# Tokens of a tile in order of their residue of sixteen, and one attention group's probabilities turned on VectorE

## What is computed

```
h = rmsnorm(x);  proj = h @ w_in
branch_a = gated retention, 4 heads (rotary, decay by distance, forward and backward)
branch_b = dilated attention, 3 groups of 8 heads of 64:
    group 1: keys at distance <= 64            (window 128,  step 1)
    group 2: keys at distance <= 256, step 4   (window 512,  step 4)
    group 3: keys at distance <= 1024, step 16 (window 2048, step 16)
    att = sum_g w_g * acc_g / sum_g w_g * l_g    (one softmax over the three)
x = x + (gate0 * branch_a + gate1 * branch_b) @ w_out
h = rmsnorm(x);  16 experts, each takes its best 64 tokens of 512 (SwiGLU), adds into x
return rmsnorm(x)
```

## Time and profile before

| | |
|---|---|
| median of 3 runs | 2398.88 us (2398.83 to 2399.2) |
| the profiled execution | 2399.03 us |
| its span, first to last instruction | 2397.2 us |
| TensorE busy | 2373.5 us (99%) |
| VectorE busy | 1588.7 us (66%) |
| ScalarE busy | 1475.4 us (62%) |
| GpSimd busy | 420.3 us (18%) |
| moved by transfers | 557.21 MB, mean 232 GB/s |
| mean granted TensorE clock | 0.997 of full speed |

### The profile page before, as it was taken

One profiled execution on the slowest core, in us unless ns is written; L12 is line 12 of the kernel. 1 busy time (PEld: TensorE's weight loads), 2 busy tenths in 40 slices (PEclk: granted clock), 3 DMA queues, 4 the chain that ended last, 5 costly groups with the idle time before them and its releaser, 6 DMA issues.

```text
span 2397.2 us, 33849 instructions
## 1 busy us (share of the span) xinstructions
PE 2373.5 (99%) x11840; PEld 1983.3 (83%) x11840; DVE 1588.7 (66%) x1737; ACT 1475.4 (62%) x1705; POOL 420.3 (18%) x287
## 2 busy tenths in 40 slices
PE   8999999999999999999998999999999999999998
PEld 7888888888888888888886888888888888888886
DVE  4444454534545454445346988888888888888887
ACT  5555564533466555544234777777777777777776
POOL 1534434000053334320002000000000000000000
PEclk9999999999999999999999999999999999999999
DMA  6413321225433224122238999999999999999998
GB/s 187 127 45 99 87 74 65 71 96 203 157 93 88 82 61 126 44 83 80 87 149 315 403 392 384 376 390 377 387 390 391 386 387 382 377 387 375 402 377 314
DMA packets 213498, 557.21 MB, mean 232 GB/s; under 512 B 10944, under 2 KB 92480, under 8 KB 208320
## 3 DMA queue, kind: packets, MB, share of 16 engines
q1 hardware_dynamic: 206384, 530.76, 60.1%
q0 software_dynamic: 7056, 25.69, 3.6%
HBM read 533.34 MB, written 23.07 MB: 232 GB/s over the span
## 4 chain that ended last, share of the span: by engine, by line
PE 98%; DVE 1%; DMA 0%; issue 0%; ACT 0%; POOLq 0%; SPq 0%; DVEq 0%; ACTq 0%
PE bank L1361 43%; PE bank L1024 15%; PE bank L1069 13%; PE bank L992 8%; PE bank L1013 6%; PE bank L1044 4%; PE bank L1183 2%; PE bank L1085 2%; PE bank L1407 2%; PE bank L1164 1%; PE bank L1107 1%; PE bank L1144 1%; PE bank L1111 1%; PE bank L1150 1%; PE bank L1241 1%; PE bank L1199 0%
## 5 line engine op out<-in xcount | busy, mean ns | idle before, releaser
L2435 DVE TENSOR_TENSOR m_lo<-m_raw,m_hi 128x2048 fp32r<-128x2048 f32 x380 | 867.6, 2291 | 122.3 <-ACT m_hi L1834 118.3
L1834 ACT ACTIVATE m_hi<-m_raw 128x2048 fp32r<-128x2048 f32 x382 | 733.5, 1921 | 262.2 <-PE bank L1361 258.1
L1361 PE MATMUL bank<-m_hi,xs_hi 128*128 128x512 f32 x1032 | 321.1, 392 | 0.0
L1361 PE MATMUL bank<-m_lo,xs_hi 128*128 128x512 f32 x1032 | 318.5, 390 | 0.0
L1361 PE MATMUL bank<-m_hi,xs_lo 128*128 128x512 f32 x1032 | 318.1, 389 | 0.0
L1972 DVE TENSOR_TENSOR w_lo<-w_raw,w_hi 128x1152 fp32r<-128x1152 f32 (+4 forms) x110 | 145.4, 1347 | 187.6 <-ACT w_hi L1489 187.5
L1361 PEld LDWEIGHTS bank<-m_hi,xs_lo 128*128 128x128 f32 x1032 | 193.7, 188 | 41.1
L1361 PEld LDWEIGHTS bank<-m_lo,xs_hi 128*128 128x128 f32 x1032 | 193.7, 188 | 40.7
L1361 PEld LDWEIGHTS bank<-m_hi,xs_hi 128*128 128x128 f32 x1032 | 191.4, 188 | 38.3 <-DVE xs_lo L2457 0.2
L1024 PE MATMUL bank<-h_hi,w_hi 128*128 128x512 f32 x512 | 202.8, 396 | 0.6
L1024 PE MATMUL bank<-h_hi,w_lo 128*128 128x512 f32 x512 | 199.4, 390 | 0.0
(11 more groups left out here) (279 smaller groups left out, 4250.1 us busy)
## 6 DMA issues: line engine op xcount, KB each, us to landing
m_raw<-in_w_exp_gate SPq DMA_DIRECT2D x128, 1024.0 KB, 9.0
m_raw<-in_w_exp_up SPq DMA_DIRECT2D x128, 1024.0 KB, 7.2
m_raw<-in_w_exp_down SPq DMA_DIRECT2D x128, 1024.0 KB, 7.7
w_raw<-in_w_b SPq DMA_DIRECT2D x66, 512.0 KB, 6.0
w_raw<-in_w_a SPq DMA_DIRECT2D x24, 1024.0 KB, 5.3
w_raw<-in_w_c SPq DMA_DIRECT2D x24, 1024.0 KB, 4.7
w_raw<-in_w_d SPq DMA_DIRECT2D x8, 1024.0 KB, 6.0
xt<-in_x SPq DMA_DIRECT2D x8, 512.0 KB, 7.8
```

What stands on the lines that cost most here:

```text
L1361: mm = pe.matmul(ps[:, half, :], a[:, chunk + k, :], v[:, k, 512 * half:512 * (half + 1)], start=first and k == n == 0, stop=last and k == ...
L1834: act.activation(m_hi[slot.slot][:, :, :], m_raw[raw.slot][:, :, :], ACT.Copy)\
L2435: dve.tensor_tensor(m_lo[slot.slot][:, :, :], m_raw[raw.slot][:, :, :], m_hi[slot.slot][:, :, :].bitcast(F32), ALU.subtract)\
```

## The change

Inside a tile the tokens are now ordered by the next two bits as well: place p of tile r holds the token at position 16 (p mod 32) + 4 (p div 32) + r. So 32 neighbouring places share one remainder of sixteen, and group 3's probabilities are nonzero only in the four 32x32 squares on the diagonal of a 128x128 block. The step `U` now transposes on TensorE only group 2, two tiles in one step (`PAIRS` = 2 steps in place of 4), and in the last of the two VectorE transposes group 3's squares where they stand, four instructions of 32 partitions by 8 squares. A new semaphore `s_squares` tells TensorE, which waits for it in `V`. The rest follows from the new order:
- `window_keys` reads group 1's keys in token order, the innermost step now going from tile to tile (128 elements apart), and `v_shifted` is loaded in token order by one transfer.
- `block_rows`, `in_blocks` and `from_tiles` have runs of 8 where runs of 32 stood.
- The exchange `I` needs two constant matrices, `same` and its transpose `back`, which comes with the retention angles: two products of 64 columns in place of one of 128.
- On the DRAM side the tokens of a tile are 4 times 32 rows (`r j m d`) where they were 128 rows with one step; this goes for `x`, `y`, `normed` and the store of `v_kept`.
- Masks, angles and distances are computed for the new order on the host.

```diff
-    order = "u W0 W1 W2 J S0 j0 J u W0 W1 W2 S1 j1 P S2 P S3 P P I P W0 P W1 T0 U0 P W2 T1 U1 P T2 U2 R0 R1"
+    order = "u W0 W1 W2 J S0 j0 J u W0 W1 W2 S1 j1 P S2 P S3 P P I P W0 P W1 T0 P W2 T1 U0 P T2 R0 R1"
...
-    extra = {0: (("T", 3), ("U", 3)), 1: (("V",), ("G", 2)), 2: (("K", 0), ("K", 1)),
+    extra = {0: (("T", 3), ("U", 1)), 1: (("V",), ("G", 2)), 2: (("K", 0), ("K", 1)),
...
-            return a.rearrange("p (r q) -> p r q", r=RES)[:, :, BLOCK * i:BLOCK * (i + 1)]
-        def by_block(a, r):
-            return a.rearrange("p (i r q) -> p r i q", i=NT, r=RES)[:, r, :, :]
+            return a.rearrange("p (g m) -> p g m", g=STEP)[:, :, RUN * i:RUN * (i + 1)]
+        def in_blocks(a):
+            return a.rearrange("p (i g m) -> p g i m", i=NT, g=STEP)
+        def from_tiles(a):
+            return a.rearrange("p (g i m) -> p g i m", g=STEP, i=NT)
         def window_keys(k, i):
-            rows = k.rearrange("p (r q) -> p r q", r=RES)[:, :, window(i):window(i) + WIN]
-            return rows.rearrange("p r (c q) -> p c r q", c=2)
+            at = window(i) // SUB
+            return k.rearrange("p (r j m) -> p m j r", r=RES, j=SUB)[:, at:at + WIN // SUB, :, :]
...
-        x_res = x.rearrange("b i p d -> b (i p) d").rearrange("b (q r) d -> b r q d", r=RES)
-        y_res, normed_res = (a.rearrange("(b q r) d -> b r q d", b=NB, r=RES) for a in (y, normed))
-        v_kept = nc.dram_tensor("v_kept", (P, RES, P), F32, kind="Internal").ap()
-        def kept_rows(r):
-            row = RES * P
-            return bass.AP(v_kept.tensor, r * P, [[row, BLOCK], [BLOCK // 2 * row, SHIFTED], [1, P]])
+        x_res = x.rearrange("b i p d -> b (i p) d").rearrange("b (m j r) d -> b r j m d", j=SUB, r=RES)
+        y_res, normed_res = (a.rearrange("(b m j r) d -> b r j m d", b=NB, j=SUB, r=RES) for a in (y, normed))
+        v_kept = nc.dram_tensor("v_kept", (T, P), F32, kind="Internal").ap()
+        kept_tokens = v_kept.rearrange("(m j r) n -> j m (r n)", j=SUB, r=RES)
+        kept_windows = bass.AP(v_kept.tensor, 0, [[P, P], [WIN0 * P, SHIFTED], [1, P]])
...
-                sp.dma_start(v_kept, v_a[:, 0, :, :]).then_inc(s_kept, 16)
+                sp.dma_start(kept_tokens, v_a[:, 0, :, :]).then_inc(s_kept, 16)
                 sp.wait_ge(s_kept, t["swap"].n() * 16 + 16)
                 apart(sp, s_apart_sp)
-                for r in range(RES):
-                    sp.dma_start(v_shifted[BLOCK * r:BLOCK * (r + 1), :, :], kept_rows(r)).then_inc(s_shifted, 16)
+                sp.dma_start(v_shifted[:, :, :], kept_windows).then_inc(s_shifted, 16)
...
-                    pe.matmul(ps_sc[:, 0, 0:P], same[:, :], spread.rearrange("p g k s c -> p (g k s c)"),
-                              start=True, stop=True).then_inc(s_swapped, 1)
+                    for side, rows in enumerate((same[:, :], back)):
+                        moved = ps_sc[:, 0, 0:P].rearrange("p (g k s c) -> p g k s c", g=NT, k=2, s=2)
+                        last = pe.matmul(moved[:, :, :, side, :], rows, spread[:, :, :, side, :], start=True, stop=True)
+                    last.then_inc(s_swapped, 1)
...
-                    r = arg[0]
-                    pe.wait_ge(s_prob, step.n(2 + 2 * r))
-                    transposes([wide[:, r, a, natural(g)] for a in range(2) for g in range(2)])
-                    if r == RES - 1:
+                    first = 2 * arg[0]
+                    pe.wait_ge(s_prob, step.n(2 + 2 * (first + 1)))
+                    transposes([wide[:, first + r, a, 0:P] for r in range(2) for a in range(2)])
+                    if arg[0] == PAIRS - 1:
                         step.k += 2 * RES
                 elif what == "V":
                     all_read(pe, s_tr_free, tr)
                     all_read(pe, s_out_free, outs)
-                    pe.wait_ge(s_shifted, t["swap"].n() * 16 * RES)
+                    pe.wait_ge(s_shifted, t["swap"].n() * 16)
+                    pe.wait_ge(s_squares, t["swap"].n())
...
-                    r = arg[0]
+                    first = 2 * arg[0]
+                    if arg[0] == PAIRS - 1:
+                        dve.wait_ge(s_prob, t["step"].n())
+                        for j in range(SUB):
+                            square = wide[BLOCK * j:BLOCK * (j + 1), :, :, P + BLOCK * j:P + BLOCK * (j + 1)]
+                            last = dve.transpose(square, square)
+                        last.then_inc(s_squares, 1)
                     dve.wait_ge(s_tr, tr.n(1))
-                    dve.tensor_copy(wide[:, r, :, :], ps_tr[:, tr.slot, :].rearrange("p (a n) -> p a n", a=2))\
+                    dve.tensor_copy(wide[:, first:first + 2, :, 0:P],
+                                    ps_tr[:, tr.slot, :].rearrange("p (r a n) -> p r a n", r=2, a=2))\
                         .then_inc(s_tr_free[tr.slot], 1)
...
+def swaps():
+    tile, block = np.arange(P)[:, None], np.arange(P)[None, :]
+    return np.where((tile // BLOCK == block // RUN % SUB) & (tile % RUN == block % RUN), 1.0, 0.0)
+def place(p):
+    return SUB * (p % BLOCK) + p // BLOCK
```

More of the change, by code:

```diff
@@ L31 @@
 AXX = mybir.AxisListType.X
+AXXY = mybir.AxisListType.XY
 P = 128
@@ L47 @@
 WIN = 2 * BLOCK
+SUB = 4
+STEP = RES * SUB
+RUN = BLOCK // SUB
+PAIRS = RES // 2
 SHIFTED = 2 * RES - 1
@@ L60 @@
 HALVES = ((0, 4), (4, 8))
-PER_HEAD = {"w": 6, "piece": 18, "proj": 16, "first": 1, "pair": 2, "turned": 2, "tr": 10, "sc": 12, "out": 6, "turn": 8, "ret": 1,
+PER_HEAD = {"w": 6, "piece": 18, "proj": 16, "first": 1, "pair": 2, "turned": 2, "tr": 8, "sc": 12, "out": 6, "turn": 8, "ret": 1,
             "score": 4, "step": 8, "link": 10, "cut": 1, "swap": 1, "raw0": 2 * NG + 1, "raw1": NG + 2}
@@ L330, in hybrid_encoder @@
         crossed = [put(f"crossed{i}", [P, T], F32)[0] for i in range(2)]
-        rope_r, _, _ = put("rope_r", [P, 2, T], F32)
+        ret_tables, _, _ = put("ret_tables", [P, 2 * T + P], F32)
+        rope_r = ret_tables[:, 0:2 * T].rearrange("p (k t) -> p k t", k=2)
+        back = ret_tables[:, 2 * T:]
         cursor[0] = area + 65536 + 256
         same, _, _ = put("same", [P, P], F32)
-        group, _, _ = put("group", [P, NT], F32)
+        group, _, _ = put("group", [P, 2, NT], F32)
         top, _, _ = put("top", [P, NT, 2, 2], F32)
@@ L2012, in share_step @@
                     last = dve.tensor_tensor(spread[:, :, :, side, :], own.unsqueeze(1).to_broadcast([P, NT, 2, 8]),
-                                             group[:, :].unsqueeze(2).unsqueeze(3).to_broadcast([P, NT, 2, 8]), ALU.mult)
+                                             group[:, 1 - side, :].unsqueeze(2).unsqueeze(3).to_broadcast([P, NT, 2, 8]), ALU.mult)
                 last.then_inc(s_spread, 1)
@@ L2016, in share_step @@
                 dve.wait_ge(s_swapped, t["swap"].n())
-                then(dve.tensor_tensor(picked.rearrange("p (m i a) -> p m i a", i=NT, a=2),
-                                       ps_sc[:, 0, 0:P].rearrange("p (m i a) -> p m i a", i=NT, a=2),
-                                       group[:, :].unsqueeze(1).unsqueeze(3).to_broadcast([P, 16, NT, 2]), ALU.mult))
+                own = group[:, :, :].rearrange("p s i -> p (s i)")
+                then(dve.tensor_tensor(picked.rearrange("p (m i a) -> p m i a", i=2 * NT, a=2),
+                                       ps_sc[:, 0, 0:P].rearrange("p (m i a) -> p m i a", i=2 * NT, a=2),
+                                       own.unsqueeze(1).unsqueeze(3).to_broadcast([P, 8, 2 * NT, 2]), ALU.mult))
                 then(dve.tensor_reduce(stats[:, 1, :, :, :, :].rearrange("p k s g a -> p g (k s) a"),
@@ L2279, in _ @@
             dve.wait_ge(s_ident, 16)
-            then(dve.reduce_sum(group[:, :], ident[:, :].rearrange("p (g q) -> p g q", g=NT), AXX))
+            then(dve.reduce_sum(group[:, 0, :], ident[:, :].rearrange("p (g q) -> p g q", g=NT), AXX))
+            then(dve.reduce_sum(group[:, 1, :], ident[:, :].rearrange("p (j g m) -> p g j m", j=SUB, g=NT), AXXY))
             then(dve.memset(aff_pad[0][:, :], 0.0))
@@ L2341, in first_column @@
                             attention_step(what, arg, HP - 1)
-                            if what == "U" and arg[0] == RES - 1:
+                            if what == "U" and arg[0] == PAIRS - 1:
                                 attention_lo(0)
@@ L2566, in rope_tables @@
     t = np.arange(T)
-    token = (RES * (t % P) + t // P).astype(f)
+    token = (RES * place(t % P) + t // P).astype(f)
     out = []
@@ L2574, in rope_tables @@
         out.append(np.stack([np.cos(angle), sign * np.sin(angle)], axis=1).astype(f))
+    out[0] = np.concatenate([out[0].reshape(P, 2 * T), swaps().T.astype(f)], axis=1)
     return out
@@ L2580, in masks @@
     row, col = np.arange(P)[:, None], np.arange(P)[None, :]
-    j, r = row % BLOCK, row // BLOCK
-    r_key, q_key = np.arange(RES)[None, :, None], np.arange(WIN)[None, None, :]
+    r, j, m = row // BLOCK, row // RUN % SUB, row % RUN
+    key = np.arange(RES * WIN)[None, :]
     near = []
```

(13 more changed lines are left out.)

22 lines of the change are left out of this document (11 added, 11 removed).

## The result

The changed kernel takes 2487.77 us, median of 4 runs (2486.76 to 2489.37), against 2398.86 for the kernel before, measured beside it: ratio 1.0376, 95% interval 1.0364 to 1.0388, slower by 89 us. The forecast was 2428, its range ended at 2440. The direction was right, the size three times too small.

The account below looks back on a forecast made before the run. TensorE was taken as the bound, busy 2373.5 of 2397.2 us. 2399.0 - 6.9 + 1.6 + 7.7 + 27 = 2428.4, forecast 2428; the likeliest case's range was 2406 to 2440, extended down to 2393.

Parts of the forecast that it names:

- part 5: Token transfers as 4 by 32 rows: only four DMA engines carry each, delaying start, seam and second closing; +27 us.
- part 1: Step U, transposes removed: two steps fewer per head, eight heads, 0.43 us each on TensorE's queue; -6.9 us.
- Part 2: Exchange I of row statistics: two products and two weight loads replace one; 0.2 us a head, +1.6 us.
- Part 3: VectorE's four square transposes per head, 0.42 us each, fit the 2.5 us left before the value products; price 0.
- Part 4: Group 1's keys read out of order, neighbours 128 elements apart: the strided read slows the key products; +7.7 us.
- Half the rate: Key products: a strided pair takes as long as 512 columns, 0.227 us; +7.7 us. Rival with even spread: 15%.
- The three terms of 9, 13 and 5: Costs in us of four-engine token loads at the start, the seam and the second closing, together +27.
- The term for the start: Opening: first weights wait behind x on one queue, delaying ScalarE's split and the first paired projection; +9 us, bounds 4 and 12.
- the record's own path: Prediction's queue at seam and second closing: residual x, then w_d, ScalarE, bank release, late projection; +13 and +5 us.
- named as a sign: Projections behind an idle TensorE running at a lower clock would make the forecast too low; no price given.
- The bounds of 14 and 36: Lowest and highest total in us for the token transfers' delays at start, seam and second closing, around +27.

## Why the prediction was wrong

**The step that failed.** It is the size of part 5, the token transfers: +27 priced, some 75 to 78 measured. The mechanism, four engines, is right. What it did to everything else on the queues and to the engines that wait was priced too low, in four ways told under part 5. A second step failed by less: part 1.

**What bounds the kernel.** "An instruction taken from TensorE's queue is worth its pitch" does not hold here. The page's 99% and the absence of waits do not show that other engines have time to spare: GpSimd's chain ended just in time. A row was there to be read, 8.92 us of `w_lo` against the distance from I to the next head.

**Part 1, -6.9.** The 0.43 us a step is right, the sum is not: about -1.7, from the two heads outside the loops. This is worked out from the pitch: six heads gain 0.86 and wait 0.86.

**Part 2, +1.6.** With the keys in runs of 8 the pitch is 104.53 against 104.28: +0.25 a head, +2.0. Right, if all of it is I; no run has I alone.

**Part 3, 0.** Right, duration (434 ns) and cover.

**Part 4, +7.7.** Near: 1.22 to 1.26 us a head, +10; the runs give +7.1 to +9.0. "Half the rate" was the right end, but partly by luck: the reason that I gave, neighbours 128 elements apart, costs 22 ns when it is tried alone.

**Part 5, +27.** The three terms of 9, 13 and 5 measured 22, 36 (40.3 less three heads) and some 21. Four omissions made that:
- The term for the start priced the split at 23.46 alone. The identity matrix stands on the same queue behind the first tile and came at 13.8 in place of 5.0, and ScalarE then waited for each later tile in turn. The opening alone is worth 19.8.
- The rate of 24.6 GB/s an engine was taken for everything on the queue. It holds where four engines work alone (86 to 108 GB/s together). But the trace has 148 GB/s with all engines busy, and issues took SyncE longer, the four new tiles at the seam 23.39 us in place of 1.75. So what stands behind the residual came some 8 us later than priced. From SyncE's issue of the residual to ScalarE's first new tile at the seam it is 45.1 us where the record has 36.6; in the second closing the split of `w_d` comes after 35.2 where it has 27.3. With these 8 us the record's own path gives TensorE's waits: 13 + 8 against 21.3, 5 + 8 against 12.5. The 32 neighbouring partitions are shown to slow 16 engines from some 412 to 237 GB/s; that they also cause the 148 here was not tried.
- The stores were set to nothing as needed "tens of microseconds later". They land after 15.2 in place of 3.2 us, ScalarE waits 7.10 us for one, and with `v_kept` they are worth 16.2, GpSimd's late work on top of VectorE's routing included.
- The lower clock behind each stall was named as a sign and priced at nothing. By TensorE's busy time it is some 16 us.

The bounds of 14 and 36 for part 5 moved only the amount of queued bytes, not their rate, and so the range ended 48 us short.

**The sum again.** -1.7 + 2.0 + 10 + 78 = +88, the measured difference of the profiled executions. This is no check of its own, since the 78 comes from the same marks. The experiments give part 5 apart from them: 68.9 came back by splitting, and splitting itself costs 6.0, so 75. Some 3 us lie between the two.

No version here that computes the whole layer beats the kernel before: with transfers and keys mended it is 2411.8, 13.1 us above it. Splitting the loads makes 6 of that, and transposes and exchange together 0.3. Near 7 us are left that no run pins to a place. In the profiled execution (14 above) the opening is 4.7 longer, the seam with its heads 5.3 and the expert stage 3.5. While GpSimd's chain, and what stands right behind it, end the head, the transposes taken away in the loops win nothing.

## What to carry to other kernels

Read a transfer's pattern twice, for the number of its slowest count (how many engines) and for the partitions that it writes at once (32 neighbours cut it from some 412 to 237 GB/s); and when one transfer slows, price everything behind it on the queue, the small constant that the first instruction needs above all, and add the lower clock behind every stall of TensorE. Before counting a removed instruction at its pitch, look for another engine's chain that ends at the same place within that amount: no wait in the profile does not mean that there is room. When a strided read replaces a dense one, look at more than its innermost step: four places 128 elements apart cost 22 ns of 280, sixteen places 32 apart 115.

## What the runs showed of the hardware, unexpected

- A moving operand (the one that TensorE streams) of 64 by 256 float32: in runs of 8 or 32 side by side 279 to 280 ns, four places 128 elements apart in turn 302, sixteen places in turn 395 to 406.
- Sixteen engines writing into 32 neighbouring partitions: 237 to 262 GB/s at a busy share of 1.03 to 1.24; transfers of the same number and size over every fourth partition 412, and 3.2 us to landing in place of 5.9.
- A store of 4 by 32 rows from GpSimd's queue: 15.2 us to landing where 128 rows took 3.2, and the queue's packets rose from 7056 to 13200; four stores of 32 rows took 2.7 us each, with 7824 packets.
- GpSimd's subtraction beside VectorE's scaling in SBUF made the latter 511 ns in place of 349, and small VectorE instructions of 0.2 us that met GpSimd's subtractions of 4.5 us ended with them, after up to 4.56 us.
- With SyncE's queue full of slow transfers, six issues of parts of a weight unit took 7.84 us in place of 3.04, and four of expert weights beside slow stores 13.67 in place of 2.22.
